# Turning the cached keys on VectorE in 32x32 blocks laid out by the gather, in a two-layer sparse-attention trunk on one Trainium2 core

## What is computed

```
k_past  = cache_k[l][page_table]     # 8 sequences x 16 pages x 128 keys, 2 KV heads x 128
v_past  = cache_v[l][page_table]
ki_past = cache_kidx[l][page_table]  # index keys, 64 wide
score = sum_h relu(qi_h . ki) * wi_h ; keep the top 256 keys of a query
s = (q . k) / sqrt(128) over the kept keys ; p = softmax(s) ; o = p v
```

## Time and profile before

| | us |
|---|---|
| median of 3 runs | 3469.86 (3469.58 to 3471.81) |
| the profiled execution's own time | 3463.73 |
| its span, first to last instruction | 3461.9 |
| PE busy | 3381.8 (98%) |
| DVE busy | 1828.8 (53%) |
| ACT busy | 1047.1 (30%) |
| POOL busy | 1238.4 (36%) |
| mean busy share of the 16 DMA engines (queue q1) | 56.7% |

### The profile page before, as it was taken

How to read it: one execution, slowest core, us unless ns; L and a number is a source line. 1 busy time by engine, 2 the same in 40 slices (tenths; PEclk the granted TensorE clock), 3 DMA queues, 4 the chain that set the end, 5 groups by cost and what they waited for, 6 DMA issues and landing times. The chain is left out here.

```text
span 3461.9 us, 66254 instructions
## 1 busy us (share of the span) xinstructions
PE 3381.8 (98%) x27454; PEld 3161.4 (91%) x27454; DVE 1828.8 (53%) x2535; ACT 1047.1 (30%) x1444; POOL 1238.4 (36%) x508
## 2 busy tenths in 40 slices
PE   5899999999999999999999999999999999999999
PEld 2699989989999989998888999898999998899998
DVE  1524468999986123342226244789989841233211
ACT  2322322223542333222223222322235423332211
POOL 0243333446324223333333333334462332234433
PEclk8899999999999999999999999999999999999999
DMA  9844444666545774658895666544332257644444
GB/s 325 283 108 117 109 112 121 188 180 200 155 133 163 232 240 157 210 194 288 289 296 177 182 174 181 141 129 114 102 112 77 84 186 237 219 149 135 131 130 95
DMA packets 591304, 593.09 MB, mean 171 GB/s; under 512 B 110876, under 2 KB 556337, under 8 KB 580923
## 3 DMA queue, kind: packets, MB, share of 16 engines
q1 hardware_dynamic: 588732, 588.59, 56.7%
q10 hardware_dynamic: 2272, 0.28, 0.1%
HBM read 546.37 MB, written 116.39 MB: 191 GB/s over the span
## 5 line engine op out<-in xcount | busy, mean ns | idle before, releaser
L869 POOL TENSOR_TENSOR w_lo_t<-raw,w_hi_t 128x1024 fp32r<-128x1024 f32 x472 | 1193.3, 2529 | 2199.4 <-ACT w_hi_t L882 2199.4
L1180 PE MATMUL acc<-act_hi,w_hi_t 128*128 128x272 f32 x6528 | 1390.0, 294 | 18.2 <-POOL w_lo_t L869 9.7
L1180 PE MATMUL acc<-act_hi,w_lo_t 128*128 128x272 f32 x6528 | 1353.0, 289 | 0.0
L1180 PE MATMUL acc<-act_lo,w_hi_t 128*128 128x272 f32 x6528 | 1349.5, 288 | 0.0
L1180 PEld LDWEIGHTS acc<-act_hi,w_hi_t 128*128 128x128 f32 x6528 | 1028.2, 189 | 77.4 <-issue 55.7
L1180 PEld LDWEIGHTS acc<-act_lo,w_hi_t 128*128 128x128 f32 x6528 | 1028.5, 189 | 0.0
L1180 PEld LDWEIGHTS acc<-act_hi,w_lo_t 128*128 128x128 f32 x6528 | 1022.6, 189 | 0.0
L882 ACT ACTIVATE w_hi_t<-raw 128x1024 fp32r<-128x1024 f32 x472 | 499.9, 1059 | 1645.1 <-PE acc L1180 1631.5
L1757 DVE SCALAR_TENSOR_TENSOR conv<-conv,cw 128x512 f32<-128x512 f32 x240 | 236.1, 984 | 13.6 <-POOL w_lo_t L869 13.6
L1180 PE MATMUL acc<-m_hi,w_hi_t 128*128 128x272 f32 x1024 | 215.2, 292 | 0.0
L1180 PE MATMUL acc<-m_lo,w_hi_t 128*128 128x272 f32 x1024 | 211.5, 287 | 0.0
(11 more groups left out here) (244 smaller groups left out, 2599.2 us busy)
## 6 DMA issues: line engine op xcount, KB each, us to landing
raw<-in_w_in_dram SPq DMA_DIRECT2D x272, 512.0 KB, 3.8
ada_ring<-in_w_ada_dram SPq DMA_DIRECT2D x95, 512.0 KB, 7.0
raw<-in_w_in_dram SPq DMA_DIRECT2D x136, 256.0 KB, 3.3
k_near<-in_cache_k_dram SPq DMA_DIRECT2D x256, 128.0 KB, 2.7
v_near<-in_cache_v_dram SPq DMA_DIRECT2D x256, 128.0 KB, 2.7
k_ring<-k_near SPq DMA_DIRECT2D x64, 512.0 KB, 5.2
v_page<-v_near SPq DMA_DIRECT2D x64, 512.0 KB, 6.4
raw<-in_w_out_dram SPq DMA_DIRECT2D x64, 512.0 KB, 4.3
```

Of the source, the lines that this page charges most:

```text
L869: pool.tensor_tensor(w_lo_t[:, m % 2], raw[:, m % 4], w_hi_t[:, m % 2].bitcast(F32), ALU.subtract).then_inc(S.w_lo, 1)
L1180: last = pe.matmul(acc[:, 2 * m + h, 0:HALF], w[:, c % 2, k, P * m:P * m + P], r[:, kt, h * HALF:(h + 1) * HALF], start=first and k == 0 a ...
```

## The change

- The gather copies a page of keys as 8 column blocks: in `k_near` each page is [head, 4 column blocks of the head, 128 keys, 32 channels]. The source is read in runs of 32 numbers (128 B), 1,024 of them for a page; the destination is contiguous.
- `load_k` puts into `k_ring` for partition (column block a, k) the keys 4k to 4k+3 of each page and head: 8 runs of 128 numbers (512 B) per partition and quarter, before 4 runs of 1 KB.
- DVE transposes each 32x32 block with one instruction per quarter (128 x 1,024 numbers), reading `k_ring` in order and writing `k_t` with a step of 4 numbers, so that keys come out in order. PE's 8 transposes, ACT's copy and DVE's copy of a quarter are gone, with `k_cp_a` and `k_cp_b`.
- `logits_s` waits for `k_turned` (now DVE's) and reads `k_t` as 4 pieces of 128 columns that are 256 numbers apart.
- Keys are gathered one page per chunk in groups 1 to 32 of each layer; values 2 pages per chunk in groups 17 to 32 of each layer; index keys of the layer itself 2 pages per chunk in groups 1 to 16 (layer 1 too). `load_kx` waits for this layer's index keys.

```diff
+def page_at(n, i):
+    return divmod(4 * (n - 1) + i, PAGES)
...
-        k_near = nc.dram_tensor("k_near", [DEPTH, SEQS, PAGES, PAGE, KVW], F32).ap()
+        k_near = nc.dram_tensor("k_near", [DEPTH, SEQS, PAGES, KVH, HD // BLK, PAGE, BLK], F32).ap()
...
-        k_ring = at(C + 16512, "k_ring", [P, 3, 4, KVW])
+        k_ring = at(C + 16512, "k_ring", [P, 3, 4 * KVH, PAGE])
...
-        k_t = at(C + 11072, "k_t", [P, 4, KVH, 512])
+        k_t = at(C + 11072, "k_t", [P, 4, 4 * KVH, PAGE])
...
-                    sp.wait_ge(S.kx_staged, 16 * DEPTH * SEQS * PAGES)
+                    sp.wait_ge(S.kx_staged, 16 * SEQS * PAGES * (l + 1))
...
-                sp.dma_start(k_ring[:, q % 3], k_near[l, b, 4 * j:4 * j + 4].rearrange("g p c -> p g c")).then_inc(k_landed[q % 3], 16)
+                src = k_near[l, b, 4 * j:4 * j + 4].rearrange("y g a (k m) i -> (a k) (y g) (m i)", m=PAGE // BLK)
+                sp.dma_start(k_ring[:, q % 3], src).then_inc(k_landed[q % 3], 16)
...
-            def gather(places, staged):
+            def gather(places, staged, keys=None):
...
+                    if keys is not None:
+                        near, cache = keys
+                        sp.dma_start(near[b, g].rearrange("h a k i -> (h a) k i"),
+                                     cache[ds(page, 1)].rearrange("y k (c i) -> (y c) k i", i=BLK)).then_inc(S.kv_staged, 16)
...
-                if l == 0 and 1 <= n < 17:
-                    gather([(x, [(kx_near[a], cache_kidx[a]) for a in range(DEPTH)]) for x in staged_at(n, i)], S.kx_staged)
-                if l == 0 and 17 <= n < 33:
-                    gather([(x, kv) for x in staged_at(n - 16, i)], S.kv_staged)
-                if l > 0 and 1 <= n < 17:
-                    gather([(x, kv) for x in staged_at(n, i)], S.kv_staged)
+                if 1 <= n < 33:
+                    gather([(page_at(n, i), [])], S.kv_staged, keys)
+                if 1 <= n < 17:
+                    gather([(x, [(kx_near[l], cache_kidx[l])]) for x in staged_at(n, i)], S.kx_staged)
+                if 17 <= n < 33:
+                    gather([(x, [values]) for x in staged_at(n - 16, i)], S.kv_staged)
...
-                            act.wait_ge(S.k_turned, q + 1)
...
-                            act.activation(k_t[:, j, 0, :], aux[:, 0, :], ACT.Copy).then_inc(S.k_cp_a, 1)
...
-            def turn_k(l, b, j):
-                q = 32 * l + 4 * b + j
-                pe.wait_ge(k_landed[q % 3], 16 * (q // 3 + 1))
...
-                        last = pe.transpose(aux[:, g, P * kk:P * kk + P], k_ring[:, q % 3, kk, g * HD:(g + 1) * HD], ident)
...
-                pe.wait_ge(S.k_cp_a, 32 * l + 4 * b + 4)
-                pe.wait_ge(S.k_cp_b, 32 * l + 4 * b + 4)
+                pe.wait_ge(S.k_turned, 32 * l + 4 * b + 4)
...
-                        pe.matmul(aux[32 * j:32 * j + 32, 2, :], q_blk[:, b, g, :], k_t[:, j, g, :], start=g == 0, stop=g == 1)
+                        pe.matmul(aux[32 * j:32 * j + 32, 2, :].rearrange("p (y n) -> p y n", n=PAGE), q_blk[:, b, g, :], k_t[:, j, g:4 * KVH:KVH, :], start=g == 0, stop=g == 1)
...
-            def keep_k(l, b, j):
-                dve.wait_ge(S.k_turned, 32 * l + 4 * b + j + 1)
+            def turn_k(l, b, j):
+                q = 32 * l + 4 * b + j
+                dve.wait_ge(k_landed[q % 3], 16 * (q // 3 + 1))
...
-                dve.tensor_copy(k_t[:, j, 1, :], aux[:, 1, :]).then_inc(S.k_cp_b, 1)
+                dve.transpose(k_t[:, j].rearrange("p x (k m) -> p x m k", m=PAGE // BLK),
+                              k_ring[:, q % 3].rearrange("p x (m i) -> p x m i", i=BLK)).then_inc(S.k_turned, 1)
```

More of the change, by code:

```diff
@@ L504, in trunk_kernel @@
             bias_done bias_stored logits_p praw_done exp_p rsum_done p_ready ptr_p ptc_p pv_p ao_p
-            k_landed0 k_landed1 k_landed2 k_turned k_cp_a k_cp_b logits_s brep_in0 brep_in1 sraw_done exp_s ps_ready pts_ps pts_done
+            k_landed0 k_landed1 k_landed2 k_turned logits_s brep_in0 brep_in1 sraw_done exp_s ps_ready pts_ps pts_done
             v_landed0 v_landed1 v_landed2 v_landed3 pv_s o_done peaks_ps peaks_done part_exp part_done part_ps w_done attn_ps ao_s
@@ L755, in aside @@
                     sp.dma_start(mask_t[:, :, :, :], table[:, T_MASK:N_TAB].rearrange("p (a b n) -> p a b n", a=2, b=SEQS)).then_inc(S.cs_in, 16)
-                kv = [(near[l], cache[l].rearrange("g p h d -> g p (h d)")) for near, cache in ((k_near, cache_k), (v_near, cache_v))]
-                if l == 0 and 1 <= n < 17:
-                    gather([(x, [(kx_near[a], cache_kidx[a]) for a in range(DEPTH)]) for x in staged_at(n, i)], S.kx_staged)
-                if l == 0 and 17 <= n < 33:
-                    gather([(x, kv) for x in staged_at(n - 16, i)], S.kv_staged)
-                if l > 0 and 1 <= n < 17:
-                    gather([(x, kv) for x in staged_at(n, i)], S.kv_staged)
+                keys, values = ((near[l], cache[l].rearrange("g p h d -> g p (h d)")) for near, cache in ((k_near, cache_k), (v_near, cache_v)))
+                if 1 <= n < 33:
[4 more added lines that the diff above has]
+                    gather([(x, [values]) for x in staged_at(n - 16, i)], S.kv_staged)
                 if 1 <= n <= N_GLU and i < 2:
@@ L1046, in window @@
                 for b in range(SEQS):
-                    for j in range(4):
-                        if h == turn_at(b, j):
-                            q = 32 * l + 4 * b + j
-                            act.wait_ge(S.k_turned, q + 1)
[L1051 to L1054, removed]
-                            act.activation(k_t[:, j, 0, :], aux[:, 0, :], ACT.Copy).then_inc(S.k_cp_a, 1)
                     if h == logits_at(b):
@@ L1366, in values_p @@
                 last.then_inc(S.pv_p, 1)
-            def turn_k(l, b, j):
-                q = 32 * l + 4 * b + j
-                pe.wait_ge(k_landed[q % 3], 16 * (q // 3 + 1))
[L1371 to L1376, removed]
-                        last = pe.transpose(aux[:, g, P * kk:P * kk + P], k_ring[:, q % 3, kk, g * HD:(g + 1) * HD], ident)
-                last.then_inc(S.k_turned, 1)
             def logits_s(l, b):
-                pe.wait_ge(S.k_cp_a, 32 * l + 4 * b + 4)
-                pe.wait_ge(S.k_cp_b, 32 * l + 4 * b + 4)
+                pe.wait_ge(S.k_turned, 32 * l + 4 * b + 4)
                 pe.wait_ge(S.q_blocked, 2 * l + 2)
@@ L1461, in window @@
                         turn_s(l, b)
-                    for j in range(4):
-                        if h == turn_at(b, j):
-                            turn_k(l, b, j)
                     if h == logits_at(b):
@@ L1968, in window @@
                         if h == turn_at(b, j):
-                            keep_k(l, b, j)
+                            turn_k(l, b, j)
                     if h == values_at(b):
```

## The result

The changed kernel takes 3448.75 us (median of 5 runs, 3443.83 to 3454.35) against 3471.81 us before (median of 5 runs, 3469.58 to 3473.68): ratio 0.9936, 95% interval 0.9922 to 0.9951. That is 23 us faster; 3413 us, 57 us faster, was forecast. The profiled execution after took 3448.75 us, its span is 3447.0 us, 14.9 us under that of before.

What follows compares the result with a forecast made beforehand. PE, busy 98% of the span, was taken as the bound; removing 64 turns takes 57 us off the profiled 3463.7 us, giving 3407, and the median's 6.1 us above that makes 3413 us, range 3403 to 3440 us.

Steps and rivals of the forecast that it cites:

- SP and the gathers: SP's issuing and the key gathers: delays covered by SP's waits for POOL; counted as nothing, 2 us as upper bound.
- PE, turns removed: Turning stages on PE: 64 turns of 0.89 us go, 57 us gained; bounds 0 and 66.
- PE, logits: Logits matmuls on PE reading four pieces of 128: no extra cost, 592 ns each; upper bound 31 us.
- rival 4: PE's time is not freed, since logits pieces and waits for the last turn take it: 3470 us, chance 0.04.
- DVE's turn: DVE's transpose of 128 x 1,024 numbers per quarter: 1.4 us, bounds 0.7 and 6.7, covered up to 4.2 us.
- Rival 3: The DVE turn is slow, 6.7 us, from the stepped write: 3504 us, chance 0.04.
- Key loads: `load_k` in 512 B packets: period's DMA rises to at most 23.1 us against 23.26 of PE; counted as nothing.
- rival 2: DMA bounds the turning stage if a 512 B packet costs 46 ns: gain only 31 us, 3439 us, chance 0.11.
- The gather in the DMA engines: Key page gathered in 1,024 packets of 128 B at 15 ns: 0.96 us, or 1.9 on eight engines; no queue.
- rival 1: The key gather fills the DMA queues, 3.84 us per page: slower, 3513 us, chance 0.07.

Runs made afterwards that it cites:

- run 3: The changed kernel with the key gather written with the 128 keys as slowest dimension instead of the 8 column blocks; 3412.31 us, ratio 0.984.
- run 6: The changed kernel with the key page in groups 1 to 16 reusing the first index page's number, one page load per chunk less; 3457.42 us, ratio 0.9967.
- run 4: The changed kernel with each key page copied as one contiguous run, leaving out the layout in column blocks; 3414.47 us, ratio 0.9843.
- run 9: Run 3 with one more page load on SP per chunk in groups 1 to 16, read and not used; 3431.88 us, ratio 0.988.
- run 10: Run 3 with two more page loads on SP per chunk in groups 1 to 16, read and not used; 3476.27 us, ratio 1.001.
- run 8: Run 3 with DVE's transpose writing its 1,024 numbers in a row, leaving out the order of the keys; 3413.14 us in one execution.

## Why the prediction was wrong

**The step that failed** is that of SP and the gathers: "SP waits 1209 / 326 = 3.7 us for POOL per chunk, so even 2 us more is covered". The reading was wrong twice. 326 counts the waits, not the chunks: over all 472 chunks it is 1209 / 472 = 2.6 us. And the row is a mean over the kernel. In the groups where the swaps are, the same query over the stretch gives 26.5 us for some 41 chunks, 0.65 us each, and in groups 2 to 6 it gives 1.7 us for some 19 chunks. The second half of the step, that what is queued behind the gather isn't among PE's waits, read the absence of a wait as slack. The swap was covered by very little; the wait it turned into (`stage`, then `q_att`) was the first thing to look for. I put 2 us at most on all of this. It measured 41 us by the milestones of the profiled executions, 36 us by their difference from run 3, and 32 us by the medians of the two kernels, each against its own kernel before.

Two sizes within the step were off as well. A key gather was put at 0.5 us to issue, the row of a contiguous one; it takes 0.79 us and holds the page load behind it for 0.48 us more. And three gathers instead of four sounded cheaper, but two of the four shared a page number with the other two: before, a chunk had two page loads and four issues; after, three and three.

**PE, turns removed:** right. 3.49 us per sequence against 3.56, 56 us in all. Run 3, a kernel that differs in the description of one DMA, is 54.7 us under the kernel before beside it, where 57 were forecast.

**PE, logits:** right, 592 ns before and after. With PE's time freed, rival 4 is out.

**DVE's turn:** forecast 1.4 us, measured 2.01; the step in the write was the part I had no row for. Within the bound of 4.2 us; one period after:

```profile
1189.12 0.61 PE L1402 MATMUL aux<-v_tok,pt_tail 32*32 32x256 f32 x2
...
1190.11 3.88 DVE L1835 STREAM_TRANSPOSE k_t<-k_ring 128x1024 f32<-128x1024 f32 x2
...
1198.86 1.92 PE L1380 MATMUL aux<-k_t,q_blk 128*32 128x512 f32 x16
```

Two turns end at 1194.0, 4.9 us before the logits that want them. Rival 3 is out.

**Key loads and rival 2:** the bound was close. A period after:

```profile
1172.00:1195.34 23.34, 23.34 (x217) 20.48 (x217) 9.07 (x10) 8.33 (x11) 7.19 (x4) 1.00 0.96 288
```

0.96 x 23.34 = 22.4 us of DMA against at most 23.1 forecast, and PE is busy throughout. Key loads land in 7.0 us instead of 5.2, and nothing waits for them but DVE before the first sequence. No gain was lost to it.

**The gather in the DMA engines and rival 1:** right in size. The DMA share of the changed kernel in 600 to 700 us is 0.66 against 0.64 before, so one key page of short runs costs what two contiguous ones do plus 0.02 x 100 / 15 = 0.13 us: 0.9 us, against 0.96. No queue filled. I expected a slower kernel from this gather only through the DMA engines; it came through the processor that issues. The Trainium skill (DMA: Bandwidth & Descriptors, Specifications) says that transfers below 512 B are read-modify-writes. By bytes the short runs are dearer here, 0.9 us for a page against 0.40 contiguous; how much of that is read-modify-write no run tells. Its other rule, that the slowest dimension of both sides sets the number of engines (same page, on why a DMA increments its semaphore by 16), would put the changed gather on eight engines and that of run 3 on sixteen. The packet counts of the two kernels, changed and then run 3, agree:

```profile
DMA packets 880078, 593.10 MB, mean 172 GB/s; under 512 B 370972, under 2 KB 849201, under 8 KB 873787
...
DMA packets 882126, 593.11 MB, mean 174 GB/s; under 512 B 373020, under 2 KB 851249, under 8 KB 875835
```

Run 3 has 2,048 small packets more, 8 for each of the 256 key gathers. Less its 262,144 short runs it has the 110,876 small packets of the kernel before, so it is the changed gather that leaves eight fewer for its semaphore. I read this as eight engines against sixteen. The two gathers also differ in SP's time, and their descriptions differ on both sides (the changed one writes one flat run of a page, run 3 writes 128 rows of 8), so whether the number of engines or the shape makes SP's wait is open.

**The median** before stands 6 to 8 us above its profiled execution and runs of one kernel spread by up to 10 us. The profiled execution after happens to be its median. So the profiled pair differs by 15 us and the medians by 23: against the 56 us won, 41 us are missing by the first and 33 by the second. The place and the cause are the same by either.

## What to carry to other kernels

Where one sequencer issues everything in a fixed order, count its time per stage as for an engine, page loads and holds between DMAs included, and read its waits over that stage: the mean over the kernel hid a stage at 0.65 us of slack per chunk, and that mean hid four groups with almost none. Check what a row counts before dividing by it. A query that returns no wait says that something is covered, not by how much. When a gather rearranges in short runs, try which dimension stands slowest before moving it: here one line was worth 32 to 36 us.

## What the runs showed of the hardware

- A DRAM to DRAM DMA of 1,024 runs of 128 B, described as 8 blocks of 128 rows, takes SP 0.79 us to issue and holds the next DMA for 1.56 us (0.50 otherwise; run 6) or the next page load for 0.76 us (0.27); described as 128 rows of 8 on both sides, 0.58 us and 0.29 us for the page load behind it (run 3); as one run, 0.51 us (run 4).
- A page load on SP, with the arithmetic and check behind it, is about 0.56 us. One more per chunk in 16 of 59 groups of a layer cost 16 us (run 9), two cost 60 (run 10).
- A 32x32 transpose on VectorE of 128 x 1,024 numbers takes 1.24 us written in a row (run 8) and 2.01 us written with a step of four numbers.
- A page of 128 KB copied DRAM to DRAM in runs of 128 B took some 0.9 us of all 16 DMA engines against 0.40 contiguous, and the gather described as 8 blocks left 8 small packets fewer for its semaphore than one described as 128 rows.
- After 4.5 us of idleness TensorE ran at the 1.2 GHz level (0.50) for the next 5 us, at 0.74 in the mean of the 5 us after that and at 1.00 behind them, which adds some 3 us to the wait (an estimate from the matmuls of these rows).
